# first loads reordered, weight splits one chunk later in the filler slots, and eight linears entered without a barrier

## The reference, cut to what matters

```python
for l in range(2):                                   # first block
    x = x + mixer_l(rms_norm(x, norm_mix[l]))        # l = 0: attention + mLSTM, gated; l = 1: neighbourhood + differential attention
    x = x + cross(rms_norm(x, ..), rms_norm(mem, ..))   # q, k normed per head, softmax, @ w_o
    x = x + conv_ffn(rms_norm(x, norm_ffn[l]))       # up, 3-tap conv, silu * value, down
for l in range(2):                                   # second block
    x = x + 0.5 * swiglu(rms_norm(x, ..))
    # hybrid mixer: three attentions (fox, sparse, stick-breaking), each projected, gated and summed
    merged = g[0] * (o_fox @ w_fox_out) + g[1] * (o_dsa @ w_dsa_out) + g[2] * (o_sb @ w_sb_out)
    x = x + merged @ w_out
    x = x + cross_2(..)                              # as above, no head norms
    x = x + 0.5 * swiglu(..)
out = rms_norm(x, final_norm)
```

## Time and profile before

| what | value |
|---|---|
| median of 3 runs | 2589.95 us (2587.48 to 2590.49) |
| the profiled execution | 2590.67 us |
| its span, first to last instruction | 2588.8 us |
| PE busy | 2394.8 us, 93% |
| DVE busy | 1603.0 us, 62% |
| ACT busy | 1096.6 us, 42% |
| mean granted TensorE clock | 0.952 of full speed |
| read from HBM | 362 MB, mean 143 GB/s |

### The profile page before, as it was taken

One profiled execution on the slowest core, in us unless ns is written; L12 is line 12 of the kernel. 1 busy time (PEld: TensorE's weight loads), 2 busy tenths in 40 slices (PEclk: granted clock), 3 DMA queues, 4 the chain that ended last, 5 costly groups with the idle time before them and its releaser, 6 DMA issues.

```text
span 2588.8 us, 41000 instructions
## 1 busy us (share of the span) xinstructions
PE 2394.8 (93%) x17744; PEld 2239.1 (86%) x17744; DVE 1603.0 (62%) x2326; ACT 1096.6 (42%) x1329; POOL 34.8 (1%) x60
## 2 busy tenths in 40 slices
PE   6989999998799999999998799999999988889997
PEld 5868899986689999999967688999999967688997
DVE  4565587755457786656557646666666446655654
ACT  4435454533444444335334345334334324445332
POOL 1300000000000000000000000000000000000000
PEclk8889999998799999999989899999999989899999
DMA  8523245441134555555521344555556522244552
GB/s 256 173 70 132 96 165 194 164 146 59 56 129 167 187 172 179 186 176 153 180 78 54 113 163 136 176 177 182 177 179 179 172 66 77 68 151 145 175 185 82
DMA packets 318901, 373.79 MB, mean 144 GB/s; under 512 B 23647, under 2 KB 289651, under 8 KB 317571
## 3 DMA queue, kind: packets, MB, share of 16 engines
q1 hardware_dynamic: 313715, 353.32, 41.7%
q0 software_dynamic: 3424, 11.50, 1.5%
q10 hardware_dynamic: 1584, 6.36, 0.7%
HBM read 361.97 MB, written 9.18 MB: 143 GB/s over the span
## 4 chain that ended last, share of the span: by engine, by line
PE 77%; DVE 11%; ACT 6%; issue 2%; PEld 2%; DMA 1%; DVEq 0%; PEldq 0%; ACTq 0%
PE bank L727 20%; PE bank L730 20%; PE bank L728 20%; DVE wlo L1503 3%; ACT whi L1140 3%; PE bank L757 2%; PE bank L758 2%; PE bank L737 2%; PE bank L968 2%; PE bank L1017 2%; PE bank L761 2%; PE bank L897 1%; PE bank L1004 1%; ACT x_hi L1186 1%; DVE xT L1532 1%
## 5 line engine op out<-in xcount | busy, mean ns | idle before, releaser
L727 PE MATMUL bank<-x_hi,wlo 128*128 128x256 f32 (+1 forms) x4432 | 1143.9, 290 | 24.3 <-DVE wlo L1503 8.3
L728 PE MATMUL bank<-x_lo,whi 128*128 128x256 f32 (+1 forms) x4432 | 1131.4, 287 | 0.0
L1503 DVE TENSOR_TENSOR wlo<-raw,whi 128x2048 fp32r<-128x2048 f32 (+2 forms) x344 | 762.0, 2224 | 324.4 <-ACT whi L1140 324.2
L1140 ACT ACTIVATE whi<-raw 128x2048 fp32r<-128x2048 f32 (+2 forms) x344 | 638.9, 1860 | 719.4 <-PE bank L730 651.5
L727 PEld LDWEIGHTS bank<-x_hi,wlo 128*128 128x128 f32 (+1 forms) x4432 | 869.5, 196 | 51.5 <-issue 31.5
L728 PEld LDWEIGHTS bank<-x_lo,whi 128*128 128x128 f32 (+1 forms) x4432 | 870.2, 196 | 0.0
L730 PE MATMUL bank<-x_hi,whi 128*128 128x256 f32 x4432 | 710.9, 286 | 0.0
L730 PEld LDWEIGHTS bank<-x_hi,whi 128*128 128x128 f32 x4432 | 615.7, 195 | 4.6 <-issue 0.7
L757 PE MATMUL bank<-x_hi,wlo 128*128 128x256 f32 x544 | 154.8, 315 | 46.5 <-DVE xT L1532 19.8
L757 PEld LDWEIGHTS bank<-x_hi,wlo 128*128 128x128 f32 x544 | 111.3, 205 | 52.2 <-issue 32.0
L758 PE MATMUL bank<-x_lo,whi 128*128 128x256 f32 x544 | 144.1, 295 | 0.0
(11 more groups left out here) (225 smaller groups left out, 1986.9 us busy)
## 6 DMA issues: line engine op xcount, KB each, us to landing
raw<-in_ffn_w_gu SPq DMA_DIRECT2D x88, 1024.0 KB, 5.1
raw<-in_ffn_w_down SPq DMA_DIRECT2D x66, 1024.0 KB, 5.2
raw<-in_ffn_w_up SPq DMA_DIRECT2D x44, 1024.0 KB, 5.1
raw<-in_w_in SPq DMA_DIRECT2D x42, 1024.0 KB, 5.2
raw<-in_ca_w_kv SPq DMA_DIRECT2D x16, 1024.0 KB, 5.1
raw<-in_od_w_in SPq DMA_DIRECT2D x12, 1024.0 KB, 5.1
raw<-in_ev_w_in SPq DMA_DIRECT2D x10, 1024.0 KB, 5.3
raw<-in_w_in SPq DMA_DIRECT2D x20, 512.0 KB, 5.2
```

The lines of the kernel that those rows point to most:

```text
L727: eng.matmul(out, a[1], b[0], start=first and i == 0, stop=False, skip_group_check=True)
L728: eng.matmul(out, a[0], b[1], start=False, stop=False, skip_group_check=True)
L1140: eng.activation(whi[s % SETS][:, 0:ch["n"]], raw[i % SLOTS][:, 0:ch["n"]], ACT.Copy).then_inc(S["weights_hi"], 1)
L1503: eng.tensor_tensor(wlo[s][:, 0:n], full[:, 0:n], whi[s][:, 0:n].bitcast(F32), ALU.subtract).then_inc(S["weights_split"], 1)
```

## The change

1. Loads: SP issues chunks 0, 1 and 2 first and the parameter rows after them. ACT's queue issues x, then the constants, then the first gains; mem is issued at the end of the first stage. GpSimd stores `na_skew` after the T5 tables and the first spill of the normed memory.
2. First stage: DVE copies the transposed x, with the split of chunk 0 after the second of four banks and that of chunk 1 after norm pair 1; ACT splits chunk 0 before all norm work. PE transposes the gains before x.
3. `fill` splits up to the unit's chunk plus 1 instead of plus 2.
4. Even mixer: the fillers in the mLSTM stage and the head norm behind it move one slot forward.
5. Barriers: the second output linears of even and odd mixer, the four cross-attention output linears and the two `w_out` linears get `join=True`. Parts are signalled by what makes them: `qk_normed` of each head (ACT rounds a head as soon as it is normed, DVE multiplies after its own norm), `att_done` for cross attention (`parts_of_heads`, which makes PE take the first two units tile by tile), and `merged` for the hybrid mixers.
6. The merge linear gets `feeds`: ACT rounds two merged tiles after each third unit, DVE makes their low parts one unit later, the last two after the loop.

```diff
+        def make_parts(src, n, buf, tile, made, per=1, by=None, scale=1.0):
+            return dict(src=src, buf=buf, tile=tile, made=made, per=per, by=by, scale=scale, count=n,
+                        m0=number("made", n if by is not None else 0), h0=number("parts", n), signal="parts_ready")
+        def parts_of_heads(at):
+            return dict(h0=at, count=0, signal="att_done")
...
-                      fill={0: (H[0], M[7]), 1: (H[1], H[0]), 3: (H[2], H[1])}, tanh=M[7] + 1)
+                      fill={"pre": (H[0], M[7]), 0: (H[1], H[0]), 1: (H[2], H[1]), 3: (H[3], H[2])}, tanh=M[7] + 1)
...
-                       fill={"pre": (H[3], H[2]), 0: (H[3] + 1, H[3]), 1: (H[3] + 1, H[3] + 1)})
+                       fill={"pre": (H[3] + 1, H[3]), 0: (H[3] + 1, H[3] + 1)})
...
+            parts = make_parts(ft[:, 18:22, :], 4, o, 4, ("qk_normed", n_of["norm_group"] - 4), by=ft[:, 14:18, :], scale=0.5)
+            return linear(residual_half(wo, o, 1), parts=parts, then=then, join=True)[-1]
...
-            linear(residual_half(wo, b, 0), then=then)
+            linear(residual_half(wo, b, 0), parts=parts_of_heads(n_of["att"] - 4), then=then, join=True)
...
+            parts = make_parts(ft[:, 0:KT, :], KT, b, 0, ("merged", number("merged", 4)), per=2, scale=0.5)
+            linear(units, tanh=G[11] + 1, feeds=parts)
+            return linear(features(io["w_out_2"][l], b, 0, D, 0, "residual", dst=None), parts=parts, then=then, join=True)[-1]
...
-            rows("norm_mix", io["norm_mix"].rearrange("l (r c) -> (l r) c", c=P), "gains_loaded")
             load(0)
+            load(1)
+            load(2)
...
-                    split_upto(units_of[emit_end - 1]["chunk"] + 2)
+                    split_upto(units_of[emit_end - 1]["chunk"] + 1)
...
             def start(st):
+                eng.dma_start(rows_in, io["x"][0].rearrange("(t p) c -> p t c", p=P)).then_inc(S["x_loaded"], 16)
                 eng.dma_start(con[:, 0:n_early], io["consts"][:, 0:n_early]).then_inc(S["consts_loaded"], 16)
+                eng.dma_start(prm[0:16, 0, :], io["norm_mix"].rearrange("l (r c) -> (l r) c", c=P)).then_inc(S["gains_loaded"], 16)
+                split_upto(0)
                 eng.wait_ge(S["cols_turned"], 1)
                 step(eng.activation(cols[:, 0:16], banks[6][:, 0:16], ACT.Copy))
                 hold()
                 for p in range(4):
                     norm_pair(st["norm"], p)
-                    if p % 2 == 0:
-                        split_upto(p // 2)
+                    if p == 1:
+                        split_upto(1)
+                eng.dma_start(mem_rows, io["mem"][0].rearrange("(t p) c -> p t c", p=P)).then_inc(S["mem_loaded"], 16)
...
                     evac_upto(un["u"] + 1)
+                    if feeds is not None and i % 3 == 2:
+                        parts_hi(feeds, 2 * (i // 3), 2 * (i // 3) + 2)
...
             def start(st):
                 eng.memset(rpt, 0.0).then_inc(S["rpt_zeroed"], 1)
+                for b in range(4):
+                    eng.wait_ge(S["x_turned"], b + 1)
+                    eng.tensor_copy(xT[:, 2 * b:2 * b + 2, :], banks[b][:, :].rearrange("p (n c) -> p n c", c=SEQ)).then_inc(S["x_copied"], 1)
+                    if b == 1:
+                        split_upto(0)
...
                     evac_upto(un["u"] + 1)
+                    if feeds is not None and i and i % 3 == 0:
+                        parts_lo(feeds, 2 * (i // 3) - 2, 2 * (i // 3))
```

More of the change, by code:

```diff
@@ L485, in odd_mixer @@
                        fill={"pre": (H[3] + 1, H[3]), 0: (H[3] + 1, H[3] + 1)})
-            parts = make_parts(ft[:, 16:20, :], 4, o, 4)
-            return linear(residual_half(wo, o, 1), parts=parts, then=then)[-1]
+            parts = make_parts(ft[:, 16:20, :], 4, o, 4, ("qk_normed", n_of["norm_group"] - 4))
+            return linear(residual_half(wo, o, 1), parts=parts, then=then, join=True)[-1]
         def cross_attention(norm, then, layer, before, wq, wkv, wo, qk_gain):
@@ L645, in _ @@
                 rows(name, io[name].rearrange("l (r c) -> (l r) c", c=P))
-            load(1)
             rows("final_norm_2", io["final_norm_2"].rearrange("(r c) -> r c", c=P))
@@ L657, in _ @@
             rows("ffn_conv_b", io["ffn_conv_b"].rearrange("l (r c) -> (l r) c", c=P))
-            for i in range(2, len(chunks)):
+            for i in range(3, len(chunks)):
                 load(i)
@@ L857, in linear @@
                     if i == 0 and (nm is not None or parts is not None):
-                        signal, at, per = ("xs_ready", KT * nm["n"], 2) if nm is not None else ("parts_ready", parts["h0"], 1)
+                        signal, at, per = ("xs_ready", KT * nm["n"], 2) if nm is not None else (parts["signal"], parts["h0"], 1)
                         pairs = [(lin_bank[n["u"] % 2], n["mms"], n["chunk"], lambda u=n["u"]: bank_free(u)) for n in units[0:2]]
@@ L1250, in norm, with parts_hi @@
                 roots_of(post_bank[0][:, 0:SEQ], rstd[:, 0, 0:SEQ], rstd2[:, 0, 0:SEQ], S["out_rs"])
-            def parts_hi(parts):
-                for k in range(parts["count"]):
+            def parts_hi(parts, first, end):
+                for k in range(first, end):
                     if parts["by"] is not None:
                         eng.wait_ge(S["parts_made"], parts["m0"] + k + 1)
+                    else:
+                        eng.wait_ge(S[parts["made"][0]], parts["made"][1] + k // parts["per"] + 1)
                     eng.activation(X[parts["buf"]][0][:, parts["tile"] + k, :], parts["src"][:, k, :], ACT.Copy, scale=parts["scale"])\
@@ L1260, in linear @@
                 nm, parts, then, units = st["norm"], st["parts"], st["then"], st["units"]
-                mem = st.get("mem")
+                mem, feeds = st.get("mem"), st.get("feeds")
                 if st.get("spread"):
@@ L1265, in linear @@
                     flush(st["tanh"])
-                if parts is not None:
-                    parts_hi(parts)
+                if parts is not None and parts["count"] == 4:
+                    parts_hi(parts, 0, 4)
                 for i, un in enumerate(units):
@@ L1541, in evac @@
                         eng.wait_ge(S["lin_free"], un["taken"])
-                        step(eng.tensor_tensor(acc, acc, g, ALU.add))
-                        hold()
+                        if b < 2:
+                            step(eng.tensor_tensor(acc, acc, g, ALU.add))
+                            hold()
+                        else:
+                            eng.tensor_tensor(acc, acc, g, ALU.add).then_inc(S["merged"], 1)
             def fill(st, slot):
@@ L1652, in norm, with parts_lo @@
                                              in1=rstd[:, 0, 0:SEQ], op0=ALU.mult, op1=ALU.mult)
-            def parts_lo(parts):
-                n, (hi, lo) = parts["count"], X[parts["buf"]]
-                for k in range(n if parts["by"] is not None else 0):
+            def parts_lo(parts, first, end):
+                hi, lo = X[parts["buf"]]
+                for k in range(first, end if parts["by"] is not None else first):
                     src = parts["src"][:, k, :]
+                    eng.wait_ge(S[parts["made"][0]], parts["made"][1] + k + 1)
                     eng.scalar_tensor_tensor(out=src, in0=parts["by"][:, k, :], scalar=1.0, in1=src, op0=ALU.add, op1=ALU.mult)\
                        .then_inc(S["parts_made"], 1)
-                for k in range(n):
+                for k in range(first, end):
                     eng.wait_ge(S["parts_hi"], parts["h0"] + k + 1)
@@ L1666, in linear @@
                 nm, parts, then, units, mem = st["norm"], st["parts"], st["then"], st["units"], st.get("mem")
-                if parts is not None:
-                    parts_lo(parts)
+                feeds = st.get("feeds")
+                if parts is not None and parts["count"] == 4:
+                    parts_lo(parts, 0, 4)
                 for i, un in enumerate(units):
```

31 lines of the change are left out of this document (11 added, 20 removed).

## The result

The changed kernel takes 2595.32 us (median of 10 runs, 2593.14 to 2597.94) against 2587.24 us before (median of 10, 2584.44 to 2590.49): ratio 1.003, 95% interval 1.002 to 1.004. It is 8.1 us slower where 1 to 2 us less were forecast, and it lies 0.3 us outside the range. The profiled executions differ by 5.4 us (spans 2594.2 and 2588.8, both with PE busy 93%).

A forecast was written before the change was run, and what follows sets the result against it. PE was taken as the bound (busy 93%), so only its idle seams could win. Start -4.5, even -1.4, odd -0.9, cross -1.1 and hybrid +1.4 gave -6.5; clock +5.1 left -1.4: forecast 2588 us, range 2580 to 2595.

The forecast's parts named there:

- the hybrid mixers, +1.4 for both: Both hybrid mixers, stick-breaking slot and merge with its join: +0.7 us each; bounds per mixer -3.5 to +2.5.
- (a): Stick-breaking attention, slot 0: a full chunk instead of 1,536 columns makes VectorE's first head 0.9 us later per hybrid mixer.
- the join gives back what the late splits cost, -0.2: Hybrid merge into output linear: removing the 3.97 us wait for parts offsets entry and late splits, net -0.2 us.
- Start, -4.5: First stage: PE reaches its second bank at 22.4 instead of 26.92 us, 4.5 earlier; bounds 3.0 to 6.3.
- L: Time when weight chunk 0 lands in the first stage: 14.3 us before, taken as 12.5, bounds 11 to 14.3.
- Even mixer, -1.4: Even mixer: fourth product 0.4 us later, head norm 1.0 earlier, no barrier 0.8 earlier; bounds +1.5 to -5.
- one unit less before the spread, 1.0 earlier: Even mixer's head norm: one unit less of PE time stands before the spread, gaining 1.0 us.
- Odd mixer, -0.9: Odd mixer's output linear: high parts made during normalization let PE start at 681.7 instead of 682.63 us, -0.9.
- Crosses, 4 x -0.27: Four cross-attention output linears: PE starts 1.07 us earlier, only 0.27 counted each, -1.1 in all; bounds 0 to -4.3.
- The clock, +5.1 for six stretches: Six PE idle stretches grow to about 2 us; each priced at half a 1.7 us fall to 1.2 GHz, +5.1.
- Rival 3: Slower: PE falls to 1.2 GHz at all four crosses and two hybrid mixers, price 20.4, 2605 us; chance 0.13.
- Rival 1: The clock does not fall and the start is good: -6.5 to -10, 2580 to 2584 us; chance 0.26.

The follow-up runs named there:

- start_joins: The whole change without the filler edits (fillers stay two chunks ahead), against the kernel before: 2582.61 us, ratio 0.9979.
- feeds_late: start_joins with ScalarE making the high parts of a merged pair after the next unit's split instead of before it: 2569.34 us, ratio 0.9939 of the kernel before.

## Why the prediction was wrong

The step that failed is **the hybrid mixers, +1.4 for both**. The trace of the changed kernel has +6.2 us for the first and +6.0 for the second (stick-breaking, merge and output linear of the table). By medians, putting the fillers back two chunks ahead there gives 6.9 us, and moving the high parts behind the split 13.1, which is more than the loss, since it also brings the gain that the feeds can have.

- **(a), the full chunk in slot 0, priced at 0.9.** The wait is 0.96 longer, as worked out. What the price left out is its consequence: the wait became 1.82 us, and PE ran at 0.50 for the next 6.8 us, 2.9 more. The part on the clock counted six places and this was none of them, though the window of rows 1 behind an equal wait of 1.82 had shown such a fall. The second mixer lost 2.5, because the kernel before fell there too, half as long. Even behind the old wait of 0.87 us, seven of 16 such stages in the other traces have a fall of 3.4 us, so 1.5 us of either number goes with the execution.
- **The merge.** The mechanism was seen (ACT waits for each merged pair before the next split), and its size is close: counted from PE's third unit, ACT's next split starts 7.2 us later in start_joins (1442.18 against 1435.00) and 5.2 in feeds_late (1438.88 against 1433.68), so 2.0 late, forecast 2.8. The error was to hold that the join gives back what the late splits cost, -0.2. In start_joins the output linear's first evacuation comes at 1483.11; with the 13.5 us that this trace is ahead when the merge begins, that is 1496.7 in the time of the kernel before, 2.5 later than its 1494.20. The second bank of the pair starts at 1472.64, which is 1486.2 in that time against the forecast 1485.4. From there the forecast counted 72 matmuls at full clock, 8.6 us, and the trace has 10.47:

```profile
1472.64:1483.11 10.47, 10.47 (x75) 10.47 (x75) 3.58 (x5) 2.52 (x3) 0.00 (x0) 0.83 0.64 202
1469.40:1476.20 6.80, 6.80 (x30) 6.21 (x29) 4.91 (x7) 2.52 (x3) 0.00 (x0) 0.50 0.75 250
...
1483.11 0.69 DVE L1541 TENSOR_TENSOR xT<-bank,xT 128x512 f32<-128x512 f32 x1 [5.07 <-PE bank L767]
```

  Merge and output linear together cost 2.9 and 3.0 in the trace of the joins alone. In the changed merge PE is at 0.82 on average; the clock term gave each mixer half a fall, 0.85 us, at the seam, and nothing inside a merge whose waits are each about 1 us.
- **The bounds.** +2.5 for each mixer "if PE falls to 1.2 GHz" was about right for the merge alone, and had no room for the stick-breaking stage beside it.

The other steps:

- **Start, -4.5 (bounds -3.0 to -6.3).** Measured 6.1 in the second bank between the two profiled executions and 5.2 on the mean of all traces. Chunk 0 landed at 11.0 (10.8 to 11.9 in the eleven traces), near the low bound of L, and the chain from there was 9.76 instead of 9.6. Right in mechanism and near in size. By itself the part gives 7.7 us; where the other 2.5 come from is open, since the half clock before 145 us is 10.2 to 27.3 us in the three traces with the old stage and 3.4 to 20.5 with the new one.
- **Even mixer, -1.4.** Measured +0.2 against the profiled execution before. First product at 161.0 in the time of the kernel before, forecast 161.0; fourth 188.2, forecast 188.5. But that execution was itself 1.5 slow here: in three other traces the unchanged chain has its fourth product at 186.6 in this time. So the earlier slots cost 1.5 there and 0.6 in the head norm, 2.2 with rounding, instead of giving 0.6, and the join gives 0.45, not 0.8. The term "one unit less before the spread, 1.0 earlier" did not come.
- **Odd mixer, -0.9.** Measured -1.0 at PE's first matmul; 0.5 is lost again within the first pair, which PE now enters 1.0 us sooner at half clock.
- **Crosses, 4 x -0.27.** Measured -0.36 at each of the four up to the feed-forward's first matmul, and a wait of 1.9 there, 2.1 forecast (its own terms, 1.51 + 1.07 - 0.27, give 2.3): right. Without the filler edit it would have been -1.25 each: the second split in DVE's queue eats two thirds of the gain.
- **The clock, +5.1 for six stretches.** Three of four crosses fell, 1.55 us each, 4.7: the right order for these places. It was short by the two stick-breaking stages and the merges. Its price came from the conv feed-forward, where a fall behind the wait of 1.82 us is repaid: the next wait there is 1.22 us instead of 2.72. Half of 1.7 us at each of six places was a guess that landed near the sum of three; no place fell half.

Rival 3 came nearest: right in sign and in mechanism, wrong in its places (three crosses, two stick-breaking stages and the merges rather than all six joins), and its 2605 too high. The forecast also stood on 2590.67 and 2589.95 us for the kernel before, whose median of ten is 2587.24; from that, the same -1.4 gives 2585.8, so the miss in the change is 9.5 us and not the 7.3 between 2588 and 2595.32. Rival 1's condition, a clock that stays whole, holds in part for the kernel with late high parts, at 2569.

Read together: the start is worth -7.7, the joins of crosses and of the even and odd mixers about -3 more (2576.9), the feeds (with the join of the `w_out` linears) -7.5 with the high parts late and +5.7 with them early, and the filler edits +12.7. The four differences come from different pairs of kernels and need not add to the digit.

## What to carry to other kernels

An operation that waits for another engine's result must not stand in front of work that was ready: here, moving two small roundings from ahead of a weight split to behind it was worth 13 us of 2595. Price a longer wait of PE with what its clock does behind it, wherever the wait falls, not only at the seams that the change is about; the wait of 0.96 us more was a loss of 3.9. A prefetch that is taken back by one chunk does not vanish: here it reappeared as longer waits in the stick-breaking stages and in front of the feed-forwards, so follow it there. And read more than one trace of the kernel before: its own half clock moved single stretches here by 1.5 to 3 us.

## What the hardware showed

- The same wait was followed by PE at 1.2 GHz at some places and not at others. In the five traces that have the wait of 1.9 us before all four feed-forwards behind a cross, there was no fall at the first of them and one of 3.4 us at each of the other three, every time. Behind the 24 waits of 1.56 or 1.57 us in six experiments (those with the crosses' fillers two chunks ahead) and the eight of 1.50 or 1.51 in two traces there was none.
- In the stick-breaking stage all ten waits of 1.82 us were followed by a fall, eight of 6.8 us and two of 3.4; behind the shorter wait of 0.87 us it was seven of 16, of 3.4 us each, at the same program point in different executions.
- Falls move: where the first wait in a conv feed-forward (1.82 us) is followed by a fall, the second is 1.2 us instead of 2.7, so that the 1.5 us lost come back. Kernels that differ only early on differ by 1.5 us in stages that are the same in both, and eleven traces with the same first stage differ by 5.6 us at 148 us.
- Products that nobody reads, put into a wait of 1.8 to 1.9 us, made the whole kernel 3.2 and 4.3 us faster.
